# Decay sums of the first model's state-space heads: stored as rows once per layer and loaded back over all partitions, in place of a spread product per head

## The reference, cut to what matters

```python
acs = jnp.cumsum(lac, axis=1)                 # decay sums of a chunk, per head
seg = acs[:, :, None] - acs[:, None, :]
lmat = jnp.where(mask, jnp.exp(jnp.where(mask, seg, 0.0)), 0.0)
cb = jnp.einsum('bign,bjgn->bijg', cc, bc)
y = jnp.einsum('bijgr,bjgrp->bigrp', cb[..., None] * lmat, xc)
y = y + jnp.einsum('bign,bgrpn->bigrp', cc, state) * jnp.exp(acs)[..., None]
```

## Time and profile before

| what | value |
|---|---|
| time, median of 3 runs | 4148.09 us (4145.03 to 4149.84) |
| profiled execution, span | 4145.5 us |
| PE busy | 3651.7 us, 88% |
| DVE busy | 2321.9 us, 56% |
| ACT busy | 657.1 us, 16% |
| POOL busy | 1280.9 us, 31% |
| HBM traffic | 1208.65 MB, mean 292 GB/s |
| granted TensorE clock, mean | 0.955 |

### The profile page before, as it was taken

The page is one execution under the profiler, slowest core; times in us unless marked ns, Lnnn a source line. Parts: engine busy times, 40 slices in busy tenths (PEclk is TensorE's granted clock), DMA queues, the critical chain, the costliest instruction groups (busy, mean ns, idle before and its releaser), DMA issues. The chain is left out here.

```text
span 4145.5 us, 41044 instructions
## 1 busy us (share of the span) xinstructions
PE 3651.7 (88%) x14584; PEld 2584.5 (62%) x14584; DVE 2321.9 (56%) x5464; ACT 657.1 (16%) x1800; POOL 1280.9 (31%) x1125
## 2 busy tenths in 40 slices
PE   8988999999989889999988989778788898877777
PEld 6666788887756778888846875333335686433332
DVE  3432011457676897775762137787763226777875
ACT  2332101110001230000002211111112211111111
POOL 1100000000664566664540003445441002444442
PEclk9999999999999899999999999999999999998899
DMA  8742344334998889998973349999996227999997
GB/s 324 283 194 88 117 151 180 134 111 145 369 411 292 295 330 395 405 389 340 413 298 125 108 152 384 415 416 401 419 415 256 103 107 288 404 420 420 418 420 331
DMA packets 207818, 1208.65 MB, mean 292 GB/s; under 512 B 23696, under 2 KB 24848, under 8 KB 96000
## 3 DMA queue, kind: packets, MB, share of 16 engines
q0 software_dynamic: 154368, 855.71, 51.5%
q1 hardware_dynamic: 53248, 350.32, 22.2%
HBM read 1204.79 MB, written 1.15 MB: 291 GB/s over the span
## 5 line engine op out<-in xcount | busy, mean ns | idle before, releaser
L1363 PE MATMUL bank<-big 128*128 128x256 f32 (+5 forms) x9848 | 2148.4, 378 | 59.5 <-issue 8.7
L1363 PEld LDWEIGHTS bank<-big 128*128 128x128 f32 (+2 forms) x9848 | 1839.0, 192 | 374.3 <-issue 67.4
L2556 POOL DMA_INDIRECT big<-in_pboth,big x1024 | 1217.5, 1189 | 1210.0 <-PE bank L1750 695.2
L1750 PE MATMUL bank<-big 128*128 128x512 f32 x2048 | 984.3, 638 | 251.2 <-ACT big L2520 251.0
L2234 DVE CUSTOM_DVE_ANT_0 big<-big 128x1024 f32<-128x1024 f32 x768 | 928.0, 1224 | 347.1 <-DMA big<-in_pboth,big 343.0
L1750 PEld LDWEIGHTS bank<-big 128*128 128x128 f32 x2048 | 407.5, 204 | 816.6 <-issue 481.4
L2543 POOL TENSOR_TENSOR big<-big 128x1 f32<-128x1 f32 (+1 forms) x49 | 37.4, 763 | 1499.4 <-DVE big L1804 1499.4
L2245 DVE SCALAR_TENSOR_TENSOR big<-big 128x1024 f32<-128x1024 f32 x254 | 326.2, 1284 | 61.3 <-DMA big<-in_pboth,big 41.5
L2520 ACT ACTIVATE big<-big 128x128 f32<-128x128 f32 x512 | 165.1, 391 | 254.9 <-DVE big L2213 248.2
L1398 PE MATMUL bank<-big 128*128 128x128 f32 x596 | 93.0, 290 | 63.5 <-ACT big L2365 20.1
L2510 ACT ACTIVATE big<-big 128x4 f32<-128x4 f32 (+2 forms) x134 | 27.7, 207 | 742.3 <-DVE big L2209 742.2
(11 more groups left out here) (203 smaller groups left out, 2177.4 us busy)
## 6 DMA issues: line engine op xcount, KB each, us to landing
big<-in_w SPq DMA_DIRECT2D x104, 1024.0 KB, 7.7
big<-in_wmod POOLq DMA_DIRECT2D x48, 1024.0 KB, 9.0
big<-in_wgu SPq DMA_DIRECT2D x44, 1024.0 KB, 8.1
big<-in_wzg SPq DMA_DIRECT2D x36, 1024.0 KB, 4.8
big<-in_wro SPq DMA_DIRECT2D x32, 1024.0 KB, 6.9
big<-in_wpq SPq DMA_DIRECT2D x24, 1024.0 KB, 6.0
big<-in_wd SPq DMA_DIRECT2D x22, 1024.0 KB, 8.4
big<-in_pboth,big POOLq DMA_INDIRECT x1024, 11.7
```

The costliest lines, as they stand in the source:

```text
L1363: last = pe.matmul(o, a, b, start=(i == 0), stop=(i == n - 1))
L1750: last = pe.matmul(u.ap, d.ap, row[:, 512 * i:512 * i + 512], start=(k == 0), stop=(k == 127))
L2556: g.indirect_dma_start(out=s.ap, out_offset=None, in_=table, in_offset=bass.IndirectOffsetOnAxis(ap=index, axis=0)).then_inc(s.full[0], 16)
```

## The change

The decay sums of all 32 heads are now also formed as rows (head on the partition, 256 tokens along it), once per layer, by three small matmuls. SP stores them in a scratch tensor in HBM and loads two heads' rows at a time back into SBUF, over all 128 partitions (a source of 2 KB read 128 times, 256 KB written). ACT reads these instead of the bank. The sums now run on through the second chunk of tokens, so that ACT's first two Relus become one and DVE's subtraction goes. `dt_sums` moves from behind c3 to between c0 and c1; the first three pairs' rows are loaded behind c1's weights, later ones with the pair three before, into a ring of four slots. A slot is free again when ACT has done the second Relu of its pair.

```diff
@@ Plan.first_block
+        sum_rows = Ring([Slot(MT[:, 2 * i:2 * i + 2, :], self.sem(f"sr{i}")) for i in range(4)])
@@ group_heads
-                    pa = self.pa2.take()
+                    rows = sums.pop(0)
+                    if 8 * g + j + 6 < 32:
+                        more_sums(8 * g + j + 6)
...
+                    seg = [tick("decay_log") for _ in range(2)]
+                    rows.free(seg[1])
@@ the layer's loop
-            yield from group_inputs(0, gots[0])
-            dts_ok = tick("dt_summed")
-            put("dt_sums", u=self.pa2.take(), dts=dts, ready=la_ok, done=dts_ok)
+            inputs = group_inputs(0, gots[0])
+            yield next(inputs)
+            dts_ok, stored = tick("dt_summed"), tick("d_sums", 16)
+            put("dt_sums", u=self.pa2.take(), dts=dts, ready=la_ok, done=dts_ok, dst=self.sums[l], stored=stored)
+            sums = []
+
+            def more_sums(h, l=l):
+                r = sum_rows.take()
+                put("load_sums", r=r, src=self.sums[l:l + 1, h:h + 2, :].rearrange("o h n -> o (h n)").to_broadcast([P, 512]), ready=stored)
+                sums.append(r)
+
+            yield next(inputs)
+            for h in (0, 2, 4):
+                more_sums(h)
+            yield from inputs
@@ PE dt_sums
-        for c in range(2):
-            pe.matmul(u.ap[:, 32 * c:32 * c + 32], umask, la[:, c, :], start=True, stop=True)
-        pe.matmul(u.ap[:, 64:96], ones, la[:, 0, :], start=True, stop=True).then_inc(u.full[0], 1)
+        pe.matmul(u.ap[:, 0:32], umask, la[:, 0, :], start=True, stop=True)
+        pe.matmul(u.ap[:, 32:64], ones, la[:, 0, :], start=True, stop=False)
+        pe.matmul(u.ap[:, 32:64], umask, la[:, 1, :], start=False, stop=True)
+        pe.matmul(u.ap[0:32, 128:256], la[:, 0, :], umask, start=True, stop=True)
+        pe.matmul(u.ap[0:32, 256:384], la[:, 0, :], ones, start=True, stop=False)
+        pe.matmul(u.ap[0:32, 256:384], la[:, 1, :], umask, start=False, stop=True).then_inc(u.full[0], 1)
@@ PE heads
-        la = by2(dts[:, 6, :])
-        opened(pa)
-        for i in range(2):
-            for c in range(2):
-                last = pe.matmul(pa.ap[:, 256 * i + 128 * c:256 * i + 128 * c + 128],
-                                 la[:, c, at + i:at + i + 1].to_broadcast([P, P]), umask, start=True, stop=True)
-        last.then_inc(pa.full[0], 1)
@@ DVE dt_sums
-        step(v.tensor_copy(D[7], u.ap[:, 0:64]))
-        v.tensor_copy(D[9][:, 0:32], u.ap[:, 64:96]).then_inc(u.free[0], 1)
-        v.wait_ge(*u.free)
-        v.tensor_tensor(D[8][:, 0:32], D[7][:, 0:32], D[9][:, 0:32], ALU.subtract).then_inc(done[0], 1)
+        v.tensor_copy(dts[:, 7, :], u.ap[:, 0:64]).then_inc(done[0], 1)
+        v.tensor_copy(dts[0:32, 0:4, :].rearrange("p a b -> p (a b)"), u.ap[0:32, 128:384]).then_inc(u.free[0], 1)
@@ ACT heads
-            s.activation(d.ap[:, 0, :], pa.ap[:, o:o + 128], ACT.Relu, bias=acs[:, 0, h:h + 1], scale=-1.0)
-            s.activation(d.ap[:, 1, :], pa.ap[:, o + 128:o + 256], ACT.Relu, bias=rel[:, h:h + 1], scale=-1.0)
-            s.activation(d.ap[:, 2, :], pa.ap[:, o + 128:o + 256], ACT.Relu, bias=acs[:, 1, h:h + 1],
-                         scale=-1.0).then_inc(seg[i][0], 1)
+            s.activation(d.ap[:, 0:2, :], row, ACT.Relu, bias=acs[:, 0, h:h + 1], scale=-1.0)
+            s.activation(d.ap[:, 2, :], row[:, 1, :], ACT.Relu, bias=acs[:, 1, h:h + 1], scale=-1.0).then_inc(seg[i][0], 1)
@@ SP
+    def dt_sums(u, dts, dst, stored, **_):
+        q.wait_ge(*u.free)
+        q.dma_start(dst, dts[0:32, 0:4, :].rearrange("p a b -> p (a b)")).then_inc(stored[0], 16)
+
+    def load_sums(r, src, ready):
+        q.wait_ge(*ready)
+        if r.before:
+            q.wait_ge(*r.before)
+        q.dma_start(r.ap.rearrange("p a b -> p (a b)"), src).then_inc(r.full[0], 16)
```

More of the change, by code:

```diff
@@ L142, in __init__ @@
         self.mods = nc.dram_tensor("mods", [2, 2, 6, 1024], F32, kind="Internal").ap()
+        self.sums = nc.dram_tensor("sums", [2, 32, 256], F32, kind="Internal").ap()
         self.big = ctx.enter_context(nc.sbuf_tensor("big", [P, BIG_N], F32))
@@ L427, in group_heads @@
                     got["cb_read"] = ahead[1][2]
-                    put("heads", pa=pa, at=8 * g + j, dd=dd, dts_ok=dts_ok, seg=[tick("decay_log"), pa.free],
+                    seg = [tick("decay_log") for _ in range(2)]
+                    rows.free(seg[1])
+                    put("heads", rows=rows, at=8 * g + j, dd=dd, dts_ok=dts_ok, seg=seg,
                         exp=[tick("decay_exp") for _ in range(2)], out=[a[2] for a in ahead], **args)
@@ L1476, in sums, with heads @@
             pe.matmul(o1, d.ap[:, 2, :], x1, start=False, stop=True).then_inc(y[0], 1)
-    def heads(ys, yp, xs, xs_ok, first, dts, pa, at, **_):
+    def heads(ys, yp, xs, xs_ok, first, **_):
         sums(ys, yp, xs, xs_ok, first)
-        la = by2(dts[:, 6, :])
-        opened(pa)
-        for i in range(2):
-            for c in range(2):
-                last = pe.matmul(pa.ap[:, 256 * i + 128 * c:256 * i + 128 * c + 128],
-                                 la[:, c, at + i:at + i + 1].to_broadcast([P, P]), umask, start=True, stop=True)
-        last.then_inc(pa.full[0], 1)
     def heads_end(ys, yp, xs, xs_ok, first, **_):
@@ L1845, in dt_sums @@
     def dt_sums(u, dts, done, **_):
-        D = [dts[:, i, :] for i in range(10)]
+        settled()
         v.wait_ge(*u.full)
-        step(v.tensor_copy(D[7], u.ap[:, 0:64]))
-        v.tensor_copy(D[9][:, 0:32], u.ap[:, 64:96]).then_inc(u.free[0], 1)
-        v.wait_ge(*u.free)
-        v.tensor_tensor(D[8][:, 0:32], D[7][:, 0:32], D[9][:, 0:32], ALU.subtract).then_inc(done[0], 1)
+        v.tensor_copy(dts[:, 7, :], u.ap[:, 0:64]).then_inc(done[0], 1)
+        v.tensor_copy(dts[0:32, 0:4, :].rearrange("p a b -> p (a b)"), u.ap[0:32, 128:384]).then_inc(u.free[0], 1)
     def conv_in(conv, **_):
@@ L2353, in xs_turn, with heads @@
             s.copy(d, turned(u, 2)).then_inc(u.free[0], 1)
-    def heads(dts, dts_ok, pa, at, dd, seg, exp, **_):
-        acs, rel = by2(dts[:, 7, :]), dts[:, 8, :]
+    def heads(dts, dts_ok, rows, at, dd, seg, exp, **_):
+        acs = by2(dts[:, 7, :])
         s.wait_ge(*dts_ok)
-        s.wait_ge(*pa.full)
+        s.wait_ge(*rows.full)
         for i, d in enumerate(dd):
-            h, o = at + i, 256 * i
+            h, row = at + i, by2(rows.ap[:, i, :])
             if d.before:
                 s.wait_ge(*d.before)
-            s.activation(d.ap[:, 0, :], pa.ap[:, o:o + 128], ACT.Relu, bias=acs[:, 0, h:h + 1], scale=-1.0)
-            s.activation(d.ap[:, 1, :], pa.ap[:, o + 128:o + 256], ACT.Relu, bias=rel[:, h:h + 1], scale=-1.0)
-            s.activation(d.ap[:, 2, :], pa.ap[:, o + 128:o + 256], ACT.Relu, bias=acs[:, 1, h:h + 1],
-                         scale=-1.0).then_inc(seg[i][0], 1)
+            s.activation(d.ap[:, 0:2, :], row, ACT.Relu, bias=acs[:, 0, h:h + 1], scale=-1.0)
+            s.activation(d.ap[:, 2, :], row[:, 1, :], ACT.Relu, bias=acs[:, 1, h:h + 1], scale=-1.0).then_inc(seg[i][0], 1)
         for i, d in enumerate(dd):
@@ L2634, in finished @@
         q.wait_ge(*stored)
[L2636 removed]
+    kinds = dict(consts=consts, load_context=load_context, block_consts=block_consts, dt_sums=dt_sums, load_sums=load_sums, mod_c=mod_c, mod_store=mod_store,
                  mods_stored=mods_stored, mod_load=mod_load, load_cs=load_cs, load_row=load_row, load_iota=load_iota,
```

## The result

The changed kernel takes 4162.06 us (median of 6 runs, 4157.1 to 4170.23), the kernel before 4145.88 us in the same runs: a ratio of 1.0043, 95% interval 1.0033 to 1.0054. It is slower by 0.4%, some 16 to 18 us, where I forecast no change to be told apart (4149) with a range of 4130 to 4168. The profiled execution is the slowest of the six, 4170.23 us.

What follows compares the result with a forecast made beforehand. PE was taken to bound the layer 0 scan and DVE the layer 1 scan. Layer 0 -6.3 and layer 1 +7.6 made +1.3, median 4149.4, said as 4149; own range 4140 to 4158, 8-in-10 range 4130 to 4168.

Steps and rivals of the forecast that it cites:

- held back pair by pair: Rival, chance 0.28: SP's wait at loads of rows delays eight conv chunks a layer by 1 to 1.5 us; 4167.
- Removed products and bank waits in layer 0: Layer 0 scan on PE: spread products -16 us, transposes' waits for the spread's bank -3.8, spread's wait for DVE's sums -0.7.
- A wait of SP in each chunk: Loads of rows wait on SP for ACT's second Relu, later weights behind; nearly always hidden, +0.5 us in layer 0.
- The hole in layer 0: Before c1, whose weights wait behind SP's store: PE idle 11.4 us plus 2.3 at the lower clock, +13.7.
- The hole in layer 1 and what DVE gets back: c1 reaches DVE 19.7 us late; DVE's earlier waits for PE shrink this to +12.7 at c4, +7.6 in all.
- PE idle before c1: Sign: PE idle about 10 us in layer 0 and some 21 in layer 1, both released by the DMA of `in_w`.
- The layer 0 scan from c1 to its end: Sign: this stretch of layer 0 becomes shorter by some 20 us.
- No transpose waits for the Relus: Sign: transposes on PE no longer wait for ACT's Relus; before, 1.47 and 2.32 us in layer 0, 6.62 in layer 1.
- over nine tenths: Sign: DVE's busy share in layer 1 behind its idle time of close to 19 us before c1's conv.
- Shallow holes: Rival, chance 0.24: loads land in about 5 us, both holes shrink by 2; layer 0 -8, layer 1 -7, 4134.
- PE as the bound of layer 1: Part of the 4134 rival, chance 0.24: PE's 35 us in layer 1 come through against 29, layer 1 -7.

Runs made afterwards that it cites:

- e4: Changed kernel without the store and all loads of rows, ACT reading constant masks instead, sums and copies kept; 0.9946 of the kernel before.
- e6: e2 with the modulation's stores also moved from SP's to ACT's queue; 4109.02 us, 0.9917 of the kernel before.
- e2: Changed kernel with the loads of rows and the store of the sums issued from ACT's queue instead of SP's; 0.9956 of the kernel before.
- e3: Changed kernel, all on SP, with the store and first three loads of rows behind c3's weights instead of around c1's; 0.9970 of the kernel before.
- e8: e2 with 2 KB instead of 256 KB per load of rows, ACT reading constant masks, all waits kept; 0.9943 of the kernel before.
- e11: e3 with the modulation's stores moved from SP's to ACT's queue; 0.9956 of the kernel before.
- e5: Kernel before, spread products kept, sums moved between c0 and c1, SP waiting for DVE's copies before c1's weights, no rows or store; 1.0055 of before.
- e1: Changed kernel with the loads of rows issued from ACT's queue, the store staying on SP; 1.0032 of the kernel before.
- e9: Changed kernel with dt_sums straight behind c0, so DVE in layer 1 copies before the context's four expert rows; 1.0018 of the kernel before.
- e7: Kernel before with only the modulation's stores moved from SP's to ACT's queue; 4140.34 us, 0.9995 of the kernel before.

## Why the prediction was right or wrong

The two holes and layer 1 came out as worked out. Layer 0's gain did not: I took it for whole, and half of it stayed behind late weights. The time, 4162, lies outside my forecast's own range (4140 to 4158) and inside the stated one only because that one reaches to the price of the rival "held back pair by pair". I had given "slower" a chance of 0.29, so that the range held is in part luck.

**Removed products and bank waits in layer 0 (-16, -3.8, -0.7): they come off, but the time does not.** I took PE to be the only bound because it was busy 52.1 of 52.1 us. e4, which keeps the new sums and drops the rows, gained 9.8 of 20.5. The step that failed is "nothing lies beside them, so that is -16". Beside them lay the landing of c10's weights, issued late behind a modulation store. In the trace before it was there already, a wait of 1.38 us at c10, hidden but for that by just the work that was taken out. e6 against e2 shows what the stores' place in SP's order costs once PE is faster: 13.8 us at the layer 0 mark. No run has e4 with those stores moved, so that they are the whole of its loss is argued from the 9.0 us of waits and slow chunk in its trace. Of the 10.7 us that are missing, 2.0 are no loss, since the products of two of the 16 pairs lie behind the mark.

**A wait of SP in each chunk, and the rows' bytes (+0.5): together 4.6 us in layer 0**, from e4 to e3 at the mark (271.19 to 275.81). The runs don't put this on the wait alone. e2, with the rows' waits off SP, stands at the same mark as e3 (275.67), and e8 puts some 5 us on the bytes there. The wait shows its own price only where the modulation's stores are gone: 12.8 us from e6 to e11. I had asked whether the rows land in time, which they do, and not what their 4 MB do to the landing of the weights beyond 0.6 us for the load ahead. And I worked with a landing of 7.4 to 9.7 us against a slack of 16.0, from medians over 70 and 100 us. The loads that matter landed after 10.6, 14.4 and 15.8 us. A median over a long window was the wrong row: in the trace before, the window 155:180 alone has

```profile
big<-in_w SPq DMA_DIRECT2D x3, 1024.0 KB, 14.5
```

and I hadn't asked for it. My rival "held back pair by pair" has this mechanism, and said for layer 0 that it decides once weights need over 9 us, which they did; but it priced eight conv chunks a layer, where two chunks of the layer were late.

**The hole in layer 0 (+13.7): right.** Between the changed kernel and e3 the mark moves by 12.7, c2 came 13.75 late, and e5 has +11.1 for the hole by itself. The chunk at the lower clock took 9.63, 2.4 us more than 7.20, where I had 2.3.

**The hole in layer 1 and what DVE gets back (+7.6): right, measured +7.8.** PE waited 19.71 us and the chain ran as worked out: DVE's idle 18.44, then c4 on PE 1384.69 in place of 1363.33 and its conv on DVE 1392.94 in place of 1372.46, of which 8.5 us came in with c0, so +12.0 on DVE for my +12.7; then the gate chunks' waits given back. That the SP waits between chunks are covered by DVE was right for this kernel: e1, which takes the rows' waits off SP, has +7.0 for the +7.8. Without the hole they cost more, 3.4 us from e2 to e3.

In sum for layer 0: -9.8 (e4) + 4.6 (e4 to e3) + 12.7 (e3 to the changed kernel) = +7.5, forecast -6.3. The steps lead from one kernel to the next, so that they add up proves nothing; what they show is where the 14 us of error in layer 0 lie. With layer 1 that is +15.4, forecast +1.3.

**Signs named in advance.** PE idle before c1 was 8.9 and 19.7 us for my 10 and 21. The layer 0 scan from c1 to its end became 3.7 us shorter (216.8 to 213.1) and not 20: this sign alone told of the missing gain. No transpose waits for the Relus, and DVE is busy 174.4 of 190 us behind c4 of layer 1 (window 1385:1575), over nine tenths as said.

**Rivals.** Shallow holes: no, e5 has both at full depth. PE as the bound of layer 1: no, e4 got 12.7 and not 35. Held back pair by pair: not in layer 1 of this kernel; in layer 0 it is part of what was missing, at two chunks.

By the Trainium skill, DMA: Bandwidth & Descriptors, section "Anatomy of one DMA — SWDGE (gpsimd) path", 1 MB would land in an estimated 4.4 us. The page fits that rule for DMAs of the gpsimd path; c1's loads here are SP's. They landed after 6.2 us (69.31 to 75.50) and 7.3 us (1351.72 to 1359.06), others after up to 15.8, and the fastest of them, e9's, after 5.1. The trace decides: as a price for a load among others the rule is far too low here.

## What to carry to other kernels

In this case a new DMA cost its queue's order before it cost bytes: ask what stands behind it in the issuing engine's list and how long each load has from issue to use; here the same bytes on another queue turned +0.4% into -0.4%, and with one more wait moved into -0.8%. When work is taken off a bound engine, list the loads whose landing it hid, with landings read at that very place and not from a median over a long window. And when two waits stand ahead of the same load, take both away before saying that neither is the cause.

## What the runs showed of the hardware

- A load of one 2 KB row over 128 partitions (256 KB) landed after 4.0 us (median of 4) at 68:76 of the changed kernel and after 8.1 (median of 12) over 100:280; the other 256 KB loads there, `in_bmod`, took 10.1 and 10.5. The store of 32 KB to HBM took 3.4 us until the loads behind it could go.
- How long a 1 MB load of SP took to land went roughly with the share of the bytes that POOL's queue moved meanwhile; the total rate was 367 to 413 GB/s in five of these six:

| load, issue to landing | us | POOL's queue, of all MB | share | GB/s |
|---|---|---|---|---|
| e9, c1 of layer 1 (1345.12 to 1350.20) | 5.1 | 0.00 of 1.24 | 0% | 244 |
| changed, c1 of layer 0 (69.31 to 75.50) | 6.2 | 0.85 of 2.33 | 36% | 376 |
| changed, c1 of layer 1 (1351.72 to 1359.06) | 7.3 | 1.51 of 2.70 | 56% | 367 |
| changed, c10 (173.60 to 184.25) | 10.6 | 3.09 of 4.40 | 70% | 413 |
| e11, c10 (156.01 to 170.37) | 14.4 | 4.33 of 5.66 | 76% | 394 |
| changed, c14 (226.28 to 242.08) | 15.8 | 4.60 of 6.28 | 73% | 397 |

  These are six loads of three traces, put side by side; no run varies POOL's loads alone. In e6, where c10's weights go out 29 us before PE takes them, PE waits for none in 50:260.
- With ACT issuing the modulation's 24 stores the time of the kernel before stayed (e7, 0.9995); with the 16 loads of rows a layer issued by ACT as well, e6 is the fastest kernel.
